# First two memory key products between the last three down products of the first feed-forward, with their results copied later

## The chip, the core and the metric

The kernel runs on one core of one Trainium2 chip. The metric is the device time of one execution in microseconds (us), and the median of several runs is compared. The core has five engines that work side by side, each through its own queue of instructions in order: TensorE (PE in the profile; its weight loads are PEld), VectorE (DVE), ScalarE (ACT), GpSimd (POOL) and SyncE (SP), which only starts transfers here. They meet through semaphores: an instruction adds to one, and another engine's queue stands still until a value is reached.

## The reference, cut to what matters

The program is a two layer hybrid block (`first_block`) and a second block with one layer (`second_block`), on 512 tokens of width 1024. All that the change touches lies in the second block's layer:

```python
def swiglu_ffn(x, w_in, w_down):
    a, b = jnp.split(x @ w_in, 2, axis=-1)
    return (jax.nn.silu(a) * b) @ w_down          # D_FF = 2816

def hybrid_layer_2(x, mem, ...):
    x = x + 0.5 * swiglu_ffn(rmsnorm(x, ffn1_norm), ffn1_w_in, ffn1_w_down)
    u = rmsnorm(x, mix_norm)
    proj = u @ w_in                               # u_ssm, q, k, v, xq, gates
    ...
    y_ssm = jax.nn.gelu(s5_scan(u_ssm, ssm_a_re, ...))
    ...
    br_mem = memory_cross_attention(xq, rmsnorm(mem, mem_norm), xattn_w_kv) @ xattn_w_up

def memory_cross_attention(xq, mem_n, w_kv):      # 256 memory rows, 4 heads of 128
    mk, mv = jnp.split(mem_n @ w_kv, 2, axis=-1)
    ...
```

The four key products `mk0` to `mk3` (one head each) and the value product `mvc0` depend on the memory alone. The mix norm depends on all eight down products of the first feed-forward.

## The kernel before

Activations lie with features on partitions: `xT` holds 8 blocks of 128 features by 512 tokens. Every float32 product is made of three rounded ones: the weight and the activation are each split into a rounded part (high) and the rest (low), and high by high, low by high and high by low are summed. A product over n blocks of 128 is thus 3n matmuls.

**The weight stream.** All weights lie in one stream of chunks of 128 x 1024, in the order of use. Three engines prepare a chunk: SP's transfer into one of RAW = 4 ring slots (`Weights.load`, L120), ACT's rounding into one of HIGH = 3 slots (`round`, L140; `round_one`, L149), POOL's subtraction in four pieces (`rest`, L170), which lie in the ring's slot. A transfer waits until the chunk four before it is used up by TensorE, a rounding until the chunk three before it is. ACT's `round(name)` stands at fixed places of ACT's queue and rounds what is due by then; `round_one` rounds one chunk, and waits for it there.

**The order around the change.** TensorE (`tensor`): eight down products `f1d0` to `f1d7`, 66 matmuls and 2.75 chunks each; behind `f1d1` the memory's sum of squares, behind `f1d5` `power_rows` (L2237), 64 small matmuls for the state space part. Then `mk0` (24 matmuls of 256 columns, one chunk), `norm_total` (the mix norm's sums over the partitions), `mk1`, `norm_spread` (its inverse root to all partitions), `mk2`, `mk3`, `mvc0` (48 matmuls, 4 chunks), `u0` to `u3` (24 matmuls, one chunk each; `u0` needs the mix norm's result), `q0`, `ssm_in`, `q1` to `q4`, `ssm_lags` (L2300, waits for DVE's `s_cw`), `q5`, and so on. Results go to two banks in turn (`proj`), and a product waits until the bank's last result is moved.

DVE (`vector`): the residual sums of the down products; `norm_scale` (L545) of the mix norm, eight times a scaling `hT` (L557) and a rest `h_low` (L551) that waits for ACT's `h_high`; then, for the state space part and without a wait on anything late, the powers of b (L3178 to L3183), `phase(0)` (L3196 to L3205), a memset and the powers of c (L3220 to L3233), the last of which raises `s_cw`; then the scan.

ACT (`scalar`): for each down product `ready(i)` rounds weights, waits for the residual sum and squares it. Then it moves `mk0`, takes the mix norm's root, and moves `mk1` to `mk3`, with two `norm_high` (L542) behind each. Then follow `round_one`, the last two `norm_high`, `mvc0`, `u0` to `u3`, and `table(0)` (L2703 to L2706), which waits for `phase(0)`.

POOL (`gpsimd`): the rests of the weights in order; behind `f1d7` it starts three transfers of 512 KB for the state space part.

The keys' place `mk` shares memory with the tail of the feed-forward's activations (`act_tail`), which the down products read to their end.

Of the kernel before, what the change touches and what calls it, by code (L numbers as in the profile page):

```python
# [10 lines left out]
ACT = mybir.ActivationFunctionType  # L11
AX = mybir.AxisListType

P = 128
T = 512
D = 1024
KD = D // P
# [56 lines left out]
class Weights:  # L74
# [109 lines left out]
    def product(self, pe, result, out, xs, tokens=False, ready=None):  # L184

        n = len(xs)
        for k, (xh, xl) in enumerate(xs):
            if ready is not None:
                ready(k)
            wh, wl = self.parts(pe, result, k)  # L190
            for i, (w, x) in enumerate(((wh, xh), (wl, xh), (wh, xl))):
                a, b = (x, w) if tokens else (w, x)
                mm = pe.matmul(out, a, b, start=(k == 0 and i == 0), stop=(k == n - 1 and i == 2))  # L193
            if (self.G.part + result, k) in self.inside:
                self.s_used.on(mm)
        self.G.close(mm)
# [164 lines left out]
def here(nc):  # L361

    return -(-nc.sbuf_base // 32) * 32
# [174 lines left out]
def norm_high(S, act, n, k):  # L538

    at = KD * NORMS.index(n)  # L540
    act.wait_ge(S.s_h.sem, at + k + 1)
    S.s_hh.on(act.activation(S.h_high[:, k, :], S.hT[:, k, :], ACT.Copy))  # L542
# [1193 lines left out]
KF = FF // P  # L1736
NP = KF - 2
X_TOTAL = 7
X_SQUARES = {j: (2 * j - 4, 2 * j - 3) for j in range(2, 6)}
X_INVERSE = {8: slice(0, HALF), 9: slice(HALF, T)}  # L1740
X_SCALE = 10
# [4 lines left out]
XH, XD, MEM = 4, 128, 256  # L1746
# [92 lines left out]
def block_tiles():  # L1839

    def ffn(n):
        t = []
        for i in range(KF):
            t += [(f"{n}a{i}", KD, P), (f"{n}b{i}", KD, P)]
        return t + [(f"{n}d{d}", KF, P) for d in range(KD)]
    t = ffn("f1") + [(f"mk{i}", KD, P) for i in range(XH)] + [("mvc0", KD, T)]
    t += [(f"{n}{i}", KD, P) for n, c in (("u", 4), ("q", 6), ("k", 6)) for i in range(c)]
    t += [("v_part0", KD, HALF)] + [(f"xq{i}", KD, P) for i in range(3)] + [("vc0", KD, T), ("xq3", KD, P)]
    for d in range(KD):
        t += [(f"g0{d}", KD, P), (f"glb{d}", 4, P), (f"gla{d}", 4, P)]  # L1850
    t += [(f"g1{d}", KD, P) for d in range(EARLY_GATES)]
    for d in range(KD):
        t += [(f"g1{d}", KD, P)] if d >= EARLY_GATES else []
        t += [(f"up{d}", 2, P), (f"g2{d}", KD, P), (f"xup{d}", 4, P)]
    return t + [(f"o{d}", KD, P) for d in range(KD)] + ffn("f2")
# [14 lines left out]
def block_groups():  # L1870

    def ffn(n, between=[]):
        g = [(f"ms_{n}", "a")] + [(f"{n}{x}{i}", OWN) for i in range(2) for x in "ab"]
        for j in range(NP):
            g += [("ms_x", OWN)] if n == "f1" and j == X_TOTAL else []
            g += [(f"{n}p{j + 2}", OWN)]
        g += [(f"{n}d0", "v"), (f"{n}d1", "v")] + between + [(f"{n}d{d}", "v") for d in range(2, KD)]
        return g if n == "f1" else g + [("ms_early", "a"), ("f2_late", OWN), ("ms_late", "a")]
    g = ffn("f1", [("ms_mem", "a")])
    g += [("mk0", "a"), ("ms_mix", "a")] + [(f"mk{i}", "a") for i in range(1, 4)] + [("mvc0", "a")]  # L1880
    g += [(f"u{i}", "a") for i in range(4)]
    g += [(f"{n}{i}", "a") for n, i in FILLERS]
    glu = [(n + str(d), e) for d in range(KD) for n, e in (("g0", "a"), ("glb", "a"), ("gla", "v"))]
    for p in range(PAIRS):
        for kind, n in DILATED[p]:
            if kind == "glu":
                g += glu[:n]
                glu = glu[n:]
            if kind == "L":
                g += [(f"lse{p}{i}", "a") for i in range(PATTERNS)]  # L1890
            if kind == "V":
                g += [(f"pv{p}{n}", "v")]
    assert not glu
    for h in range(XH):
        g += [(f"g1{h}", "a"), (f"xo{h}", "v")]
    for d in range(KD):
        g += [(f"g1{d}", "a")] if d >= EARLY_GATES else []
        g += [(f"up{d}", "v"), (f"g2{d}", "a"), (f"xup{d}", "v")]
    g += [(f"o{d}", "v") for d in range(KD)]
    g += ffn("f2")  # L1900
    return g

# [5 lines left out]
def second_block(nc, stack, S, A, scratch, out_dram, first_lead, spent):  # L1908
# [16 lines left out]
    xT, hT, h_parts, rstd, proj, att, G, W = S.xT, S.hT, S.h_parts, S.rstd, S.proj, S.att, S.G, S.W  # L1925
    vecs, halfpi, epsc = S.vecs, S.halfpi, S.eps
    s_a, s_v, s_ac, s_vc = S.s_a, S.s_v, S.s_ac, S.s_vc
# [5 lines left out]
    v = qkvx[:, 12:18, :].rearrange("p a b -> p (a b)").rearrange("p (a b) -> p a b", a=TB)  # L1933
    xq = qkvx[:, 18:22, :]
    mk_at, mk = here(nc), sb("mk", [P, XH, MEM])
    logits_at, logits = here(nc), sb("logits", [P, LALL])
# [9 lines left out]
    merged = big[:, 4:4 + KD, :]  # L1946
    memT = logits[:, T:T + KD * MEM].rearrange("p (a b) -> p a b", a=KD)
    memsq = nc.alloc_sbuf_tensor_at("b2_memsq", [P, KD, MEM], F32, offset=S.h_high_at)
    mem_root = hT[:, 0, 0:MEM]
    x_squares = qkvx[:, 14:14 + KD, :]  # L1950
    x_rstd = rstd[:]
# [51 lines left out]
    mem_low = rounded("mem_low", [P, KD, MEM], logits_at + 4 * T)  # L2003
    mem_high = rounded("mem_high", [P, KD, MEM], turned_at)
# [24 lines left out]
    def act_rest(i):  # L2029
# [22 lines left out]
    s_gh, s_gl, s_memh, s_meml, s_bh, s_bl, s_mgh, s_mgl = (sem(n) for n in (  # L2052
        "act_high act_low mem_high mem_low branch_high branch_low merged_high merged_low").split())
# [60 lines left out]
    def tensor(pe):  # L2114
# [19 lines left out]
        def pair_products(n):  # L2134

            for j in range(NP):
                if n == "f1" and j == X_TOTAL:
                    G.open(pe, "ms_x")
# [49 lines left out]
        def ffn(n, norm_name):  # L2188
            lead_product(S, pe, norm_name, f"{n}a0", 0, lead[n], f"ms_{n}")
            lead_product(S, pe, norm_name, f"{n}b0", 1, lead[n], f"ms_{n}")  # L2190
            lead_product(S, pe, norm_name, f"{n}a1", 2, lead[n], f"ms_{n}")
            lead_product(S, pe, norm_name, f"{n}b1", 3, lead[n], f"ms_{n}")
            pair_products(n)
            xs = [(act_high[:, i, :], act_rest(i)) for i in range(KF)]
            pe.wait_ge(s_gated.sem, s_gated.base + 2 * pair_of(n, NP - 2) + 2)
            base = 0 if n == "f1" else KF
            for d in range(KD):
                ready = (lambda i: pe.wait_ge(s_gl.sem, base + i + 1)) if d == 0 else None
                if (n, d) == ("f2", KD - 1):
                    last_products(xs)  # L2200
                    continue
                product(f"{n}d{d}", xs, ready)
                if n == "f1" and d == 1:
                    memory_sum()
                if n == "f1" and d == 5:
                    power_rows()

        def half_total(i):

# [27 lines left out]
        def power_rows():  # L2237

            pe.wait_ge(s_r.sem, 3)
            for block in range(BLOCKS):  # L2240
                for i, at in enumerate((19, 14)):
                    for q_ in range(4):
                        j = 4 * block + q_
                        mm = pe.matmul(att[i][32 * q_:32 * q_ + 32, block * P:(block + 1) * P],
                                       st[:, at, j:j + 1].to_broadcast([P, 32]), ident, start=True, stop=True)
            s_arow.on(mm)
# [7 lines left out]

        ffn("f1", "ffn1")

        pe.wait_ge(s_meml.sem, KD)
        mem_parts = [(mem_high[:, j, :], mem_low[:, j, :]) for j in range(KD)]
        for i in range(XH):
            product(f"mk{i}", mem_parts)  # L2260
            if i == 0:
                norm_total(S, pe, "mix", "ms_mix")
            if i == 1:
                norm_spread(S, pe, "mix")
        banks = [G.open(pe, "mvc0"), att[2]]
        for k_, (xh, xl) in enumerate(mem_parts):
# [274 lines left out]
    def scalar(act):  # L2541

        G.part = "b."
        def move(name, out, func=ACT.Copy, src=None, **kw):
            W.round(act, name)
            bank = G.whole(act, name)
            G.empty(act.activation(out, bank[:, :] if src is None else src(bank), func, **kw), name)
# [128 lines left out]
        pair_ffn("f1", "ffn1")  # L2676
        memory()
        def ready(i):
            W.round(act, f"f1d{i}")
            G.moved(act, f"f1d{i}")  # L2680
        norm_squares(S, act, "mix", ready)
        half = lambda b: b[:, 0:HALF]

        move("mk0", mk[:, 0, :], src=lambda b: b[:, 0:MEM])
        norm_root(S, act, "mix", "ms_mix")
        for i in range(1, XH):
            move(f"mk{i}", mk[:, i, :], src=lambda b: b[:, 0:MEM])
            norm_high(S, act, "mix", 2 * i - 2)
            norm_high(S, act, "mix", 2 * i - 1)
        W.round_one(act)  # L2690
        norm_high(S, act, "mix", 6)
        norm_high(S, act, "mix", 7)
        W.round(act, "mvc0")
        bank = G.whole(act, "mvc0")
        s_ac.on(act.activation(mv[:, 0, :], bank[:, :], ACT.Copy))
# [31 lines left out]
        for m, (n, i) in enumerate(FILLERS):  # L2727
# [12 lines left out]
            else:  # L2740
                g = 0 if n == "xq" else i // 2
# [62 lines left out]
        for p in range(PAIRS):  # L2804
            d = 4 * p
# [1063 lines left out]
```

## Time and profile before

| what | value |
|---|---|
| median of 3 runs | 2422.01 us (2421.76 to 2422.35) |
| the profiled execution, its own time | 2421.36 us |
| its span in the profile | 2419.3 us |
| TensorE busy | 2396.3 us, 99% of the span |
| VectorE busy | 1358.7 us, 56% |
| ScalarE busy | 1151.4 us, 48% |
| GpSimd busy | 1359.0 us, 56% |
| mean granted TensorE clock | 0.998 |

The times of a row are counted from the start of the span. A row's duration of a matmul includes the time to pass through the array and overlaps the next one; what a matmul costs in a row of them is the distance of the starts. In square brackets behind an instruction stands how long its engine was idle ahead of it, and what ended that.

### The profile page before, as it was taken

To read this page: it belongs to the slowest core of one execution; us is meant where nothing else is said; L and a number is where in the kernel's file an instruction comes from. 1 tells how busy PE (TensorE), PEld (TensorE's weight loads), DVE (VectorE), ACT (ScalarE), POOL (GpSimd) and SP (SyncE) were. 2 spreads that over 40 slices of the span, in tenths; PEclk is the share of its full clock that TensorE was granted. 3 is DMA by queue.
4 is the path that set the end of the run, shared out by engine and by line. 5 is a ranking of instruction groups with operands and counts; after the bars stand their busy time and mean duration, and the time that the engine had idled before them with its cause. 6 is when DMAs were issued, how large, how long until landed. Compare 5 with 4: busy or idle time off the path is not lost.

```text
span 2419.3 us, 36056 instructions
## 1 busy us (share of the span) xinstructions
PE 2396.3 (99%) x13834; PEld 2036.7 (84%) x13834; DVE 1358.7 (56%) x2527; ACT 1151.4 (48%) x1825; POOL 1359.0 (56%) x1774
## 2 busy tenths in 40 slices
PE   9999999999999999999999999999999999999998
PEld 6887788888788787888889998878988788899987
DVE  7965865222696576432387753199266433766502
ACT  5444676323534477532366553242366524555521
POOL 5553554555564454455586774584443455877753
PEclk9999999999999999999999999999999999999999
DMA  4232221233232212232223332332222233233332
GB/s 151 92 119 78 71 78 63 96 97 98 85 96 84 79 62 79 79 96 96 97 89 104 105 122 89 130 114 79 82 84 71 70 97 96 88 106 105 105 96 88
DMA packets 64423, 224.59 MB, mean 93 GB/s; under 512 B 7367, under 2 KB 10951, under 8 KB 64124
## 3 DMA queue, kind: packets, MB, share of 16 engines
q1 hardware_dynamic: 62620, 216.49, 28.0%
q0 software_dynamic: 1632, 5.78, 0.7%
q8 instruction: 111, 1.82, 0.3%
q14 instruction: 60, 0.49, 0.1%
HBM read 219.57 MB, written 3.99 MB: 92 GB/s over the span
## 4 chain that ended last, share of the span: by engine, by line
PE 90%; DVE 4%; POOL 3%; ACT 2%; DMA 1%; issue 1%; SPq 0%; DVEq 0%; ACTq 0%; POOLq 0%
PE proj L193 62%; PE proj L2157 9%; PE att L2157 7%; PE att L193 2%; PE proj L913 1%; PE att L892 1%; POOL b_x_low L3517 1%; PE att L1004 1%; POOL weight_low L170 1%; PE att L903 1%; PE att L991 1%; PE att L2346 1%; PE att L946 1%; POOL weight_low L3511 1%; DMA ring<-in_stream 1%; PE att L935 1%
## 5 line engine op out<-in xcount | busy, mean ns | idle before, releaser
L170 POOL TENSOR_TENSOR weight_low<-ring,weight_high 128x256 fp32r<-128x256 f32 x1272 | 999.7, 818 | 902.2 <-ACT weight_high L140 882.4
L193 PE MATMUL proj<-h_high,weight_high 128*128 128x512 f32 x1320 | 520.2, 394 | 0.7 <-POOL weight_low L170 0.6
L193 PE MATMUL proj<-h_low,weight_high 128*128 128x512 f32 x1320 | 514.1, 389 | 0.0
L193 PE MATMUL proj<-h_high,weight_low 128*128 128x512 f32 x1320 | 513.9, 389 | 0.0
L140 ACT ACTIVATE weight_high<-ring 128x1024 fp32r<-128x1024 f32 x313 | 329.7, 1054 | 302.8 <-PE proj L193 264.9
L193 PEld LDWEIGHTS proj<-h_high,weight_high 128*128 128x128 f32 x1320 | 247.8, 188 | 57.0 <-issue 4.2
L193 PEld LDWEIGHTS proj<-h_low,weight_high 128*128 128x128 f32 x1320 | 247.8, 188 | 52.2
L193 PEld LDWEIGHTS proj<-h_high,weight_low 128*128 128x128 f32 x1320 | 248.0, 188 | 49.4
L3511 POOL TENSOR_TENSOR weight_low<-ring,weight_high 128x256 fp32r<-128x256 f32 x240 | 191.6, 826 | 0.0
L193 PE MATMUL proj<-b_act_high,weight_high 128*128 128x512 f32 (+1 forms) x352 | 135.0, 384 | 0.0
L193 PE MATMUL proj<-b_act_high,weight_low 128*128 128x512 f32 (+1 forms) x352 | 134.7, 383 | 0.0
L1643 DVE TENSOR_TENSOR turned<-proj,probs 128x512 f32<-128x512 f32 x32 | 22.1, 692 | 189.4 <-PE proj L193 189.4
L2157 PE MATMUL proj<-b_x_T_high,h_low 128*128 128x256 f32 x640 | 119.1, 284 | 3.8 <-issue 3.8
L2990 DVE SCALAR_TENSOR_TENSOR xT<-proj,xT 128x512 f32<-128x512 f32 x15 | 10.4, 692 | 186.8 <-PE proj L193 186.8
L193 PE MATMUL proj<-b_act_low,weight_high 128*128 128x512 f32 (+1 forms) x288 | 110.2, 383 | 0.0
L3527 POOL TENSOR_TENSOR hT<-ring 128x256 f32<-128x256 f32 x80 | 58.2, 748 | 90.7 <-PE proj L2157 90.7
L2157 PEld LDWEIGHTS proj<-b_x_T_high,h_low 128*128 128x128 f32 x640 | 100.1, 193 | 4.2 <-issue 4.2
L2157 PE MATMUL proj<-b_x_T_low,h_low 128*128 128x256 f32 x320 | 90.8, 284 | 0.0
L193 PE MATMUL proj<-weight_high,h_high 128*128 128x256 f32 x288 | 82.4, 286 | 0.0
L193 PE MATMUL proj<-weight_high,h_low 128*128 128x256 f32 x288 | 81.5, 283 | 0.0
L193 PE MATMUL proj<-weight_low,h_high 128*128 128x256 f32 x288 | 81.5, 283 | 0.0
L193 PEld LDWEIGHTS proj<-b_act_high,weight_high 128*128 128x128 f32 x352 | 66.1, 188 | 13.1 <-issue 0.2
(618 smaller groups left out, 5636.9 us busy)
## 6 DMA issues: line engine op xcount, KB each, us to landing
ring<-in_stream SPq DMA_DIRECT2D x398, 512.0 KB, 3.5
xT<-in_x SPq DMA_DIRECT2D x4, 512.0 KB, 6.3
idx<-gate_rows POOLq DMA_DIRECT2D x8, 256.0 KB, 4.0
out<-hT SPq DMA_DIRECT2D x8, 256.0 KB, 2.3
bias_rows<-bias_row SPq DMA_DIRECT2D x2, 512.0 KB
b_logits<-in_mem POOLq DMA_DIRECT2D x1, 1024.0 KB, 5.0
bias_rows<-bias_row SPq DMA_DIRECT2D x1, 768.0 KB
consts<-in_const SPq DMA_DIRECT2D x1, 576.0 KB, 9.6
```

The source lines that it names most:

```text
L140: self.s_high.on(act.activation(self.high[:, c % HIGH, :], self.raw[:, c % self.slots, :], ACT.Copy))
L170: self.s_low.on(pool.tensor_tensor(self.low[:, c % self.slots, cols], self.raw[:, c % self.slots, cols], self.high[:, c % HIGH, cols], ALU ...
L193: mm = pe.matmul(out, a, b, start=(k == 0 and i == 0), stop=(k == n - 1 and i == 2))
L892: mm = pe.matmul(att[2 * bank + hh][:, col:col + WQ[b]], dq[rows(hh), p, b * P:(b + 1) * P], dk[rows(hh), p, 0:WQ[b]], start=True, stop=True)
L903: tr = pe.transpose(att[2 * bank + hh][:, col + (b - s) * P:col + (b - s + 1) * P], probs[:, hh, OQ[b] + s * P:OQ[b] + (s + 1) * P], ident)
L913: mm = pe.matmul(out[rows(hh), s * P:T], v[:, s, h * HD:(h + 1) * HD], turned[:, hh, KOFF[s]:KOFF[s] + WK[s]], start=(s == 0), stop=(s == ...
L935: mm = pe.matmul(att[3 * hh + bank][:, col:col + WQ[b]], sq_[rows(hh), p, b * P:(b + 1) * P], sk[rows(hh), p, 0:WQ[b]], start=True, stop=True)
L946: tr = pe.transpose(att[3 * hh + bank][:, col + (b - s) * P:col + (b - s + 1) * P], probs[:, hh, at:at + P], ident)
L991: mm = pe.matmul(att[3 * (h % 2) + bank][:, col:col + WK[s]], mk[:, h, s * P:(s + 1) * P], mq[:, h, s * P:T], start=True, stop=True)
L2157: mm = pe.matmul(out, w[:, cols], part[:, k, :], start=(first and k == 0 and i == 0), stop=(k == 3 and i == 2), skip_group_check=True)
L3511: signal.on(pool.tensor_tensor(out[:, cols], form[:, cols], high[:, cols], ALU.subtract))
L3527: s_sf3.on(pool.tensor_tensor(s_slot(3 * q_ + 1)[2][:, cols], W.raw[:, ca % RAW, cols], W.raw[:, cb % RAW, cols], ALU.subtract))
```

## The change

The weights of `mk0` are put behind those of `f1d5` in the stream, those of `mk1` behind `f1d6`, and the products stand there in TensorE's order; the other two keys stay behind `f1d7`. `power_rows` moves from behind `f1d5` to behind `f1d4`. The wait for the memory's rests (`s_meml`) moves ahead of `mk0`. ACT moves the two early results to `mk_early`, a free place in `logits`, and copies both to `mk` in one instruction behind the mix norm's root. `norm_total` now stands behind `mk2`, `norm_spread` behind `mk3`. On ACT, one `round_one` now stands ahead of all eight `norm_high`, and two more between them.

```diff
+EARLY_KEYS = {5: 0, 6: 1}
@@ block_tiles
-        return t + [(f"{n}d{d}", KF, P) for d in range(KD)]
-    t = ffn("f1") + [(f"mk{i}", KD, P) for i in range(XH)] + [("mvc0", KD, T)]
+        for d in range(KD):
+            t += [(f"{n}d{d}", KF, P)]
+            t += [(f"mk{EARLY_KEYS[d]}", KD, P)] if n == "f1" and d in EARLY_KEYS else []
+        return t
+    t = ffn("f1") + [(f"mk{i}", KD, P) for i in range(len(EARLY_KEYS), XH)] + [("mvc0", KD, T)]
@@ block_groups
-        g += [(f"{n}d0", "v"), (f"{n}d1", "v")] + between + [(f"{n}d{d}", "v") for d in range(2, KD)]
+        for d in range(KD):
+            g += [(f"{n}d{d}", "v")] + (between if d == 1 else [])
+            g += [(f"mk{EARLY_KEYS[d]}", "a")] if n == "f1" and d in EARLY_KEYS else []
-    g += [("mk0", "a"), ("ms_mix", "a")] + [(f"mk{i}", "a") for i in range(1, 4)] + [("mvc0", "a")]
+    g += [("mk2", "a"), ("ms_mix", "a"), ("mk3", "a"), ("mvc0", "a")]
@@ second_block
+    mk_early = logits[:, T + KD * MEM:T + KD * MEM + 2 * MEM].rearrange("p (a b) -> p a b", a=2)
@@ tensor, ffn
-                if n == "f1" and d == 5:
+                if n == "f1" and d == 4:
                     power_rows()
+                if n == "f1" and d in EARLY_KEYS:
+                    if d == min(EARLY_KEYS):
+                        pe.wait_ge(s_meml.sem, KD)
+                    product(f"mk{EARLY_KEYS[d]}", mem_parts)
@@ tensor
-        pe.wait_ge(s_meml.sem, KD)
-        for i in range(XH):
+        for i in range(2, XH):
             product(f"mk{i}", mem_parts)
-            if i == 0:
+            if i == 2:
                 norm_total(S, pe, "mix", "ms_mix")
-            if i == 1:
+            if i == 3:
                 norm_spread(S, pe, "mix")
@@ scalar
         def ready(i):
+            if i - 1 in EARLY_KEYS:
+                m = EARLY_KEYS[i - 1]
+                move(f"mk{m}", mk_early[:, m, :], src=lambda b: b[:, 0:MEM])
             W.round(act, f"f1d{i}")
             G.moved(act, f"f1d{i}")
         norm_squares(S, act, "mix", ready)
-        move("mk0", mk[:, 0, :], src=lambda b: b[:, 0:MEM])
+        move("mk2", mk[:, 2, :], src=lambda b: b[:, 0:MEM])
         norm_root(S, act, "mix", "ms_mix")
-        for i in range(1, XH):
-            move(f"mk{i}", mk[:, i, :], src=lambda b: b[:, 0:MEM])
-            norm_high(S, act, "mix", 2 * i - 2)
-            norm_high(S, act, "mix", 2 * i - 1)
+        G.moved(act, "mk1")
+        s_ac.on(act.activation(mk[:, 0:2, :], mk_early, ACT.Copy))
+        move("mk3", mk[:, 3, :], src=lambda b: b[:, 0:MEM])
         W.round_one(act)
-        norm_high(S, act, "mix", 6)
-        norm_high(S, act, "mix", 7)
+        for t in range(KD):
+            norm_high(S, act, "mix", t)
+            if t in (2, 5):
+                W.round_one(act)
```

## Rows read from the trace of the kernel before

**Rows 1.** The page, first part: busy time of each engine.

```profile
PE 2396.3 (99%) x13834; PEld 2036.7 (84%) x13834; DVE 1358.7 (56%) x2527; ACT 1151.4 (48%) x1825; POOL 1359.0 (56%) x1774
```

**Rows 2.** Busy time by stretch: length; PE, PEld, DVE, ACT, POOL; granted clock; DMA share.

```profile
1546.00:1562.00 16.00, 16.00 (x74) 13.28 (x73) 1.48 (x3) 3.26 (x4) 8.48 (x12) 1.00 0.29 99
1575.00:1590.00 15.00, 12.88 (x51) 8.79 (x51) 14.76 (x22) 7.11 (x10) 15.00 (x16) 1.00 0.43 144
```

**Rows 3.** Timeline of TensorE, from the first key product to the value product.

```profile
1561.55 0.28 PE L193 MATMUL proj<-b_mem_high,weight_high 128*128 128x256 f32 x1
...
1564.42 0.95 PE L516 MATMUL proj<-consts_all,rstd 128*128 128x1 f32 x8
...
1568.18 1.05 PE L524 MATMUL att<-consts_all,scal 128*128 128x128 f32 x8
...
1574.82 0.40 PE L2270 MATMUL proj<-weight_high,b_mem_high 128*128 128x512 f32 x1
```

**Rows 4.** The same timeline: the longest of five waits in the value product, and its end.

```profile
1579.05 0.50 PE L2270 MATMUL proj<-weight_high,b_mem_high 128*128 128x512 f32 x1 [0.86 <-POOL weight_low L170]
...
1589.44 0.39 PE L193 MATMUL proj<-h_high,weight_high 128*128 128x512 f32 x1
```

**Rows 5.** The chain that ended last, in order of time: start, length, what.

```profile
1564.62 6.86 DMA ring<-in_stream
...
1572.64 13.86 POOL weight_low L170 x14
1589.60 27.20 PE proj L193 x120
```

**Rows 6.** Timeline of ACT at the mix norm, and at the first table.

```profile
1570.05 1.29 ACT L542 ACTIVATE h_high<-hT 128x512 fp32r<-128x512 f32 x2 [1.29 <-DVE hT L557]
1571.50 1.06 ACT L140 ACTIVATE weight_high<-ring 128x1024 fp32r<-128x1024 f32 x1 [0.16 <-DMA ring<-in_stream]
...
1611.89 1.05 ACT L2703 ACTIVATE b_big<-b_big 128x1024 f32<-128x1024 f32 x1
```

**Rows 7.** Timeline of POOL, the rests of the weights behind the keys.

```profile
1572.64 28.98 POOL L170 TENSOR_TENSOR weight_low<-ring,weight_high 128x256 fp32r<-128x256 f32 x32 [2.83 <-ACT weight_high L140]
...
1617.40 8.95 POOL L170 TENSOR_TENSOR weight_low<-ring,weight_high 128x256 fp32r<-128x256 f32 x8 [4.03 <-ACT weight_high L140]
```

**Rows 8.** Busy time by stretch, as rows 2, cut at the stages of DVE's chain.

```profile
1569.25:1580.75 11.50, 10.44 (x66) 8.61 (x65) 11.28 (x16) 9.32 (x14) 8.67 (x9) 1.00 0.57 189
1580.75:1593.90 13.15, 12.08 (x50) 9.17 (x51) 12.98 (x19) 4.16 (x5) 13.15 (x16) 1.00 0.40 132
1593.90:1611.00 17.10, 17.10 (x78) 14.14 (x77) 16.59 (x27) 4.64 (x6) 14.27 (x18) 1.00 0.30 93
1612.70:1616.50 3.80, 3.80 (x19) 3.05 (x17) 3.73 (x8) 3.77 (x5) 0.67 (x1) 1.00 0.71 268
1616.50:1640.55 24.05, 24.05 (x218) 20.29 (x217) 23.81 (x25) 6.88 (x9) 19.25 (x18) 1.00 0.30 89
1664.90:1677.80 12.90, 12.90 (x170) 10.85 (x169) 12.76 (x27) 2.13 (x3) 5.94 (x8) 1.00 0.25 83
```

**Rows 9.** Timelines of DVE (state scalars, end of the powers of c) and of TensorE (`ssm_lags`).

```profile
1490.78 0.85 DVE L2944 TENSOR_TENSOR b_st<-b_st 128x16 f32<-128x16 f32 x2
...
1639.36 1.23 DVE L3233 TENSOR_TENSOR b_big<-b_big,b_qkvx 128x512 f32<-128x512 f32 x1
...
1642.50 1.95 PE L2307 MATMUL att<-b_big,b_qkvx 128*32 128x128 f32 x64
```

**Rows 10.** Timeline of TensorE behind its two longest idle times of one kind.

```profile
1232.11 0.48 PE L2157 MATMUL proj<-b_x_T_high,h_low 128*128 128x256 f32 x2 [1.90 <-issue]
...
2086.63 0.47 PE L2157 MATMUL proj<-b_x_T_high,h_low 128*128 128x256 f32 x2 [1.91 <-issue]
```

**Rows 11.** Busy time by stretch behind these two idle times, as rows 2.

```profile
1233.00:1237.00 4.00, 4.00 (x23) 4.00 (x22) 2.93 (x4) 1.33 (x2) 4.00 (x4) 0.57 0.01 4
...
2086.00:2090.00 4.00, 3.37 (x28) 3.40 (x29) 3.27 (x5) 2.14 (x5) 4.00 (x4) 1.00 0.02 4
```

More of the change, by code:

```diff
@@ L2204, in ffn @@
                     memory_sum()
-                if n == "f1" and d == 5:
+                if n == "f1" and d == 4:
                     power_rows()
+                if n == "f1" and d in EARLY_KEYS:
+                    if d == min(EARLY_KEYS):
+                        pe.wait_ge(s_meml.sem, KD)
+                    product(f"mk{EARLY_KEYS[d]}", mem_parts)
+        mem_parts = [(mem_high[:, j, :], mem_low[:, j, :]) for j in range(KD)]
         def half_total(i):
@@ L2255, in tensor @@
         ffn("f1", "ffn1")
-        pe.wait_ge(s_meml.sem, KD)
-        mem_parts = [(mem_high[:, j, :], mem_low[:, j, :]) for j in range(KD)]
-        for i in range(XH):
+        for i in range(2, XH):
             product(f"mk{i}", mem_parts)
-            if i == 0:
+            if i == 2:
                 norm_total(S, pe, "mix", "ms_mix")
-            if i == 1:
+            if i == 3:
                 norm_spread(S, pe, "mix")
```

## The prediction, made before the changed kernel was run

> **What bounds the kernel now.** The page's first part comes first: TensorE is busy for 2396.3 of 2419.3 us [rows 1], so all its waits together are worth 23 us. What the change is worth must be read from the stage that it edits. In the table by stretch, TensorE is full in the last down products (16.00 of 16.00 us), while in the value product behind them it works 12.88 of 15.00 us and POOL all 15.00 [rows 2]. The timeline gives the same wait in another way: `mvc0` lasts from 1574.82 to 1589.44 [rows 3, 4], 14.62 us. Its 48 matmuls cost 27.20 / 120 = 0.227 us each where nothing is late [rows 5], 10.88 us in all. So 3.7 us are lost there, in five waits for POOL, the longest 0.86 us [rows 4]. The chain that ended last says why: the transfer of the first value chunk took 6.86 us, and from 1572.64 the chain runs through POOL [rows 5], which needs 28.98 / 8 = 3.62 us for a chunk [rows 7] of which TensorE uses one in 10.88 / 4 = 2.72 us.
>
> Then comes the engine that seems far from critical. By stretch, DVE is busy without a break from the mix norm at 1569.25 to 1640.55: 11.28 of 11.50, 12.98 of 13.15, 16.59 of 17.10, 3.73 of 3.80 and 23.81 of 24.05 us [rows 8]. Its last instruction ends at 1639.36 + 1.23 = 1640.59, and `ssm_lags`, which needs it, starts on TensorE at 1642.50 [rows 9]. The chain has 1.9 us to spare, and no wait shows that today.
>
> **Part by part.** I write times of the changed kernel less the shift of the eighth down product's end as "shifted", to set them beside rows of before.
>
> *The moved products.* A key product takes 1564.42 - 1561.55 = 2.87 us [rows 3], the same in either place, since TensorE has no gaps in the downs [rows 2]: the end of `f1d7` moves 5.74 us later, and 5.74 us less work follows it. The wait for the memory's rests and the earlier `power_rows` cost nothing: DVE has finished both inputs by 1490.78 + 0.85 = 1491.6 [rows 9], some 20 us ahead of either. The result banks alternate as before, and a bank's move is covered by a key product or a down product.
>
> *The stall in the value product.* The first two value chunks are now rounded as `mk2` and `mk3` were, and POOL has both done by 1570 shifted, ahead of their use. The third takes the first one's place in time: its transfer waits for `mk2`, lands at 1571.48 shifted [rows 5], and POOL starts on it at 1572.64. TensorE, which starts `mvc0` at about 1569.0 (shifted, two keys earlier), uses the first two until 1574.5. It finds the first half of chunk three just done (two pieces of 3.62 / 4 us, 1574.45), waits some 0.4 us for the second half and as much for each half of chunk four, since 2.72 us of use stand against 3.62 us of POOL's. With the restarts I take 1.5 of the 3.7 us as left and 2.2 us as gained.
>
> *The vector chain.* It starts behind `norm_spread`, which stands behind two key products and `f1d7` as before. So it starts 5.74 us later, whatever the value product gains. Four terms follow.
> (1) Start: +5.74.
> (2) The norm's rests wait for ACT. Before, the first `h_high` ran at 1570.05, ahead of the rounding at 1571.50 that waited for the 6.86 us transfer [rows 6]. Now `round_one` stands ahead of all eight, and the first `h_high` starts at about 1571.50 + 1.06 = 1572.56. DVE has two scalings done by then and 14 of its 16 instructions of 11.50 / 16 = 0.72 us [rows 8] before it: 1573.2 + 10.1 = 1583.3 against 1580.75. The bounds are 0 and +2.5; I take +2.2, near the upper one, since DVE can't begin a rest sooner.
> (3) The powers of b (13.15 us under full POOL work [rows 8]) stay as they are. `phase` runs faster with less POOL work beside it: it takes 17.10 us with 14.27 us of POOL, its twin 12.90 us with 5.94 [rows 8], 0.50 us for each us of POOL. It would start at about 1596.1 shifted. POOL then has six chunks behind 1572.64 instead of eight, is done with them at 1595 and with the two of `q0` and `q1` at 1598 and 1603 (ACT rounds them when `u1` and `u2` are done): 5.4 us beside the phase, 12.6 us long, with the 0.4 us gap ahead of the memset 13.0. That is -4.1; the bounds are -7.1 (no POOL at all) and 0.
> (4) ACT's `table(0)`, at 1611.89 [rows 6] the first to wait for the phase, starts some 3 us later and holds up the roundings of `q2` and on. POOL's work on five chunks, from 1617.40 at 8.95 / 8 = 1.12 us a piece [rows 7], falls wholly into the powers of c: 22.4 us instead of 0.67 + 19.25 [rows 8], times 0.50: +1.2. The bounds are 0 and +2.5.
> The sum is 5.74 + 2.2 - 4.1 + 1.2 = +5.0. The chain ends at 1645.6, and `ssm_lags` starts 5.0 - 1.9 = 3.1 us later than before. TensorE would be there 2.2 us earlier, at 1640.3, and stands idle for 5.3 us: the gain in the value product is given back in full, with 3.1 us more. The rounding behind the table feeds `q2`, at 1623.7 by TensorE's new order, and is some 0.7 us early; if it were late, only the wait at `ssm_lags` would be shorter.
>
> *What comes behind.* From there the order is as before and shifted for both engines, for DVE 1.9 us more than for TensorE; I find no place there where DVE is needed within that. The copy of both keys, one ACT instruction of half a microsecond, lies in ACT's wait for the transfer. The end moves with `ssm_lags`.
>
> *The clock.* The trace has no idle time of 5 us in its middle. It has two of 1.9 us: behind the one that ends at 1232.11 the granted clock was 0.57 on average over 4.00 us, the lower level of 1.2 GHz for most of it; behind the one that ends at 2086.63 it stayed at 1.00 [rows 10, 11]. The first cost up to 4.00 x 0.43 = 1.7 us. For an idle time over twice as long I take 1.7; the bounds are 0 and 3.4, twice that. The Trainium skill ("TensorE: Matmul & The Clock Gate", Part 1: The HAM clock gate) says that an idle TensorE is put back to half its clock and gets the full one only after sustained work. By that rule the cost would fall due at `ssm_lags` and the sum would be that with it; the trace agrees in one of the two idle times.
>
> The sum is 3.1 + 1.7 = +4.8 us on the execution's own 2421.36, which gives 2426.2. The median of the runs is 0.65 us above that execution, so the forecast for a median is 2426.8.
>
> **Rivals.**
> A. The forecast: DVE's chain sets the start of `ssm_lags`, and the clock falls. 2426.8. For it: the chain without breaks [rows 8] and 1.9 us of slack [rows 9]. Against it: each of its terms beyond the first is an estimate.
> B. The same wait, but the clock stays up, as at 2086.63 [rows 11]: 2425.1. A wait this long speaks against it.
> C. Faster: DVE catches up. With little POOL work beside it, `phase` and the powers of c shrink until `s_cw` is there when TensorE arrives, at 1640.3; then the value product's 2.2 us stay, and the time is 2419.8. This decides from a chain that ends at least 0.3 us earlier than before's 1640.59, so terms 2 to 4 would have to make -6.0 where I count -0.7. At 0.50 us for each us, all of POOL's work beside both stages is worth some 17 us, so it can't be excluded, but the weights of `q0` to `q4` have to be made in that time.
> D. Clearly slower: POOL's relief in `phase` fails to come, as its two chunks for `q0` and `q1` or late ones of `u` fall into it after all. Then term 3 is about -1, the chain ends 8.1 us late, TensorE waits 6.2 us more than before, and with the clock the time is 2429.9.
> E. The moved products change neither: the wait for weights goes elsewhere by the same amount and DVE is not needed in time. 2422.0. The five waits for POOL [rows 4] and the moved norm speak against it.
>
> **How the numbers follow.** Chances: A 0.56, B 0.15, C 0.12, D 0.13, E 0.04. The forecast is A's, 2426.8. The range takes in B and D's middle and the bounds of the clock: 2423.0 to 2430.5; C, E and the far end of D stay outside, with some 0.2. About 0.2% is what a measurement of this kernel can tell from no change, that is 4.8 us, and A lies on that line: half of it counts as slower. Slower: 0.28 + 0.13 = 0.41. Faster by that much needs more than all of the 3.7 us in the value product: 0.02 of C. The same: the rest, 0.57.
>
> **What would show it.** In the changed kernel's profile: TensorE in `mvc0` with about 1.5 us of waits instead of 3.7; an idle time of 4 to 7 us ahead of `ssm_lags`, ended by DVE's last power of c, and this link in the chain that ended last; DVE without a break from the norm to it, its `phase` some 4 us shorter; ACT waiting for a transfer ahead of the first `h_high`; a granted clock below 1.00 in `ssm_lags` and `q5`. The prediction is wrong if TensorE has no wait at `ssm_lags` (C or E), or if a wait of more than 1 us shows in the downs, where I count none.

## The result, and the profile after

The changed kernel takes **2427.57 us** (median of 11 runs, 2426.97 to 2428.73), the kernel before 2421.76 us (2420.95 to 2422.35) beside it: a ratio of 1.0025, with an interval of 1.0017 to 1.0033. The change costs 5.8 us; the forecast was 2426.8 us, that is 4.8 us. The profiled execution is the longest of the eleven, 2428.73 us, span 2426.8 us.

Two rows place it against the rows of before. They are TensorE's idle times of 1.9 us of [rows 10], far ahead of the edit and far behind it.

Timeline of TensorE, changed kernel (start, length, engine, line, operation, tiles; in brackets the idle time before it and what ended it):

```profile
1233.00 0.47 PE L2164 MATMUL proj<-b_x_T_high,h_low 128*128 128x256 f32 x2 [1.90 <-issue]
...
2094.00 0.47 PE L2164 MATMUL proj<-b_x_T_high,h_low 128*128 128x256 f32 x2 [1.90 <-issue]
```

The first stands 1233.00 - 1232.11 = 0.89 us later than in [rows 10], the second 2094.00 - 2086.63 = 7.37 us. This execution thus brings 0.89 us along from ahead of the edit, and loses 6.48 us between the two. From here, "net" means less 0.89 us.

The same view at the start and the end of the value product, and at `ssm_lags`:

```profile
1575.66 0.47 PE L2281 MATMUL proj<-weight_high,b_mem_high 128*128 128x512 f32 x1
...
1584.57 0.50 PE L2281 MATMUL proj<-weight_high,b_mem_high 128*128 128x512 f32 x1 [0.18 <-POOL weight_low L170]
1586.41 0.50 PE L2281 MATMUL proj<-weight_high,b_mem_high 128*128 128x512 f32 x1 [0.17 <-POOL weight_low L170]
1589.01 0.47 PE L193 MATMUL proj<-h_high,weight_high 128*128 128x512 f32 x1 [0.96 <-POOL weight_low L170]
...
1647.49 3.64 PE L2318 MATMUL att<-b_big,b_qkvx 128*32 128x128 f32 x64 [5.23 <-DVE b_big L3248]
...
1651.65 0.63 PE L193 MATMUL proj<-h_high,weight_low 128*128 128x512 f32 x1
...
1657.42 3.85 PE L2305 MATMUL att<-b_uT,b_qkvx 32*128 32x128 f32 x128
```

And `ssm_in(1)` in the kernel before, beside [rows 9]:

```profile
1650.05 3.85 PE L2294 MATMUL att<-b_uT,b_qkvx 32*128 32x128 f32 x128
```

The value product begins at 1575.66 and `u0` at 1589.01: 13.35 us against 14.62 [rows 3, 4], 1.27 us gained. From `u0` to `ssm_lags` it is 58.48 us against 1642.50 - 1589.44 = 53.06 [rows 4, 9]: 5.42 us lost, and the row says to what: TensorE stood idle for 5.23 us until DVE's last power of c. `ssm_lags` itself lasts 3.64 us in place of 1.95 [rows 9], and a matmul of 128x512 right behind it takes 0.63 us. From `ssm_lags` to `ssm_in(1)` it is 9.93 us, against 1650.05 - 1642.50 = 7.55 in the kernel before: 2.38 us more. The filled wait below, where the clock is full, has 7.55 us too. The sum, -1.27 + 5.42 + 2.38 = 6.53, is the 6.48 us between the two markers.

Busy time by stretch, changed kernel (length; PE, PEld, DVE, ACT, POOL, each with its instructions; granted clock; DMA share, GB/s):

```profile
1590.60:1603.80 13.20, 13.20 (x60) 10.92 (x59) 13.03 (x19) 4.98 (x7) 13.20 (x16) 1.00 0.29 88
1603.80:1616.50 12.70, 12.70 (x60) 10.25 (x59) 12.26 (x27) 2.42 (x4) 7.68 (x10) 1.00 0.38 125
1616.50:1647.40 30.90, 25.75 (x224) 21.52 (x224) 30.52 (x32) 11.79 (x14) 22.61 (x20) 0.97 0.28 86
1640.00:1647.00 7.00, 2.25 (x10) 1.52 (x9) 6.90 (x9) 0.60 (x1) 4.35 (x4) 0.91 0.28 75
1647.00:1651.00 4.00, 3.51 (x64) 2.96 (x64) 4.00 (x13) 0.00 (x0) 0.00 (x0) 0.50 0.00 0
1651.00:1653.00 2.00, 2.00 (x9) 1.59 (x6) 1.97 (x7) 1.76 (x3) 0.00 (x0) 0.60 0.00 0
1653.00:1657.00 4.00, 4.00 (x19) 3.32 (x18) 3.97 (x5) 1.67 (x3) 2.21 (x3) 1.00 0.00 0
```

The first three rows are stages of DVE's chain, as in [rows 8]: DVE is busy in nearly all of each, and POOL works for 7.68 us beside the phase in place of 14.27. The last four are the clock: 0.50 for the four microseconds behind the idle time, the lower level of 1.2 GHz, and 1.00 again from 1653.

Timeline of DVE, changed kernel: the norm, then the starts of the powers of b, of the phase and of the memset behind it, and the last power of c:

```profile
1575.94 1.41 DVE L557 SCALAR_TENSOR_TENSOR hT<-xT,vecs_all,att 128x512 f32<-128x512 f32 x2 [2.72 <-PE att L524]
1579.41 0.82 DVE L551 TENSOR_TENSOR h_low<-hT,h_high 128x512 fp32r<-128x512 f32 x1 [2.07 <-ACT h_high L542]
1580.16 0.73 DVE L557 SCALAR_TENSOR_TENSOR hT<-xT,vecs_all,att 128x512 f32<-128x512 f32 x1
1580.82 1.26 DVE L551 TENSOR_TENSOR h_low<-hT,h_high 128x512 fp32r<-128x512 f32 x1
...
1584.51 1.25 DVE L551 TENSOR_TENSOR h_low<-hT,h_high 128x512 fp32r<-128x512 f32 x1
...
1586.34 0.68 DVE L551 TENSOR_TENSOR h_low<-hT,h_high 128x512 fp32r<-128x512 f32 x1
...
1590.62 0.67 DVE L3193 TENSOR_TENSOR b_qkvx<-b_qkvx,att 128x512 f32<-128x512 f32 x1
...
1603.81 3.52 DVE L3211 TENSOR_SCALAR b_turned<-consts_all,b_st 128x128 f32<-128x128 f32 x8
...
1616.57 1.76 DVE L3223 MEMSET b_logits<- 128x2048 f32 x1 [0.37 <-issue]
...
1646.75 0.69 DVE L3248 TENSOR_TENSOR b_big<-b_big,b_qkvx 128x512 f32<-128x512 f32 x1
```

And of ACT, where that 2.07 us wait comes from, and of POOL, up to the end of the phase:

```profile
1577.80 1.06 ACT L149 ACTIVATE weight_high<-ring 128x1024 fp32r<-128x1024 f32 x1 [2.37 <-DMA ring<-in_stream]
1578.77 1.14 ACT L542 ACTIVATE h_high<-hT 128x512 fp32r<-128x512 f32 x2
```

```profile
1578.94 7.42 POOL L170 TENSOR_TENSOR weight_low<-ring,weight_high 128x256 fp32r<-128x256 f32 x8 [2.47 <-ACT weight_high L149]
1588.11 17.85 POOL L170 TENSOR_TENSOR weight_low<-ring,weight_high 128x256 fp32r<-128x256 f32 x20 [1.75 <-ACT weight_high L149]
1607.27 3.38 POOL L170 TENSOR_TENSOR weight_low<-ring,weight_high 128x256 fp32r<-128x256 f32 x4 [1.31 <-ACT weight_high L140]
1610.59 2.20 POOL L3520 DMA_DIRECT2D b_big<-bias_rows  x3
```

The chain that ended last, changed kernel (start, length, what):

```profile
1571.29 6.49 DMA ring<-in_stream
1577.80 1.06 ACT weight_high L149
1579.41 0.82 DVE h_low L551
...
1646.75 0.70 DVE b_big L3248
1647.49 3.64 PE att L2318 x64
1651.13 6.36 PE proj L193 x24
```

In [rows 5] the chain went from the transfer to POOL and from POOL to TensorE at `u0`. Now it goes from the transfer of the third value chunk, which stands in the first one's place, to ACT's rounding, to the norm's first rest, and through DVE alone for 68 us, until it reaches TensorE at `ssm_lags`. The engine that had 1.9 us to spare has become the bound of this stretch.

### The profile page after: what moved, and what is told of

The parts are those of the page before. It is cut to its first block, busy times and chain, and to the rows that moved or that the text cites. A ratio compares the mean times of both kernels' runs of the same rounds, so it can differ in the third digit from the quotient of the medians.

```text
span 2426.8 us, 36057 instructions
## 1 busy us (share of the span) xinstructions
PE 2397.4 (99%) x13834; PEld 2037.2 (84%) x13834; DVE 1358.3 (56%) x2527; ACT 1152.8 (48%) x1826; POOL 1360.0 (56%) x1774
## 3 DMA queue, kind: packets, MB, share of 16 engines
q0 software_dynamic: 1632, 5.78, 0.8%
## 4 chain that ended last, share of the span: by engine, by line
PE 88%; DVE 7%; POOL 2%; ACT 2%; DMA 1%; issue 1%; SPq 0%; DVEq 0%; ACTq 0%; POOLq 0%
PE proj L193 60%; PE proj L2164 9%; PE att L2164 7%; PE att L193 2%; PE proj L913 1%; PE att L892 1%; POOL b_x_low L3532 1%; PE att L1004 1%; PE att L903 1%; PE att L991 1%; PE att L2357 1%; POOL weight_low L3526 1%; PE att L946 1%; DMA ring<-in_stream 1%; PE att L935 1%
```

## The experiments

Each time is a median of 11 or 12 runs, with the interval of its ratio to the kernel before (2421.63 us beside the first four, 2421.48 beside the next four, 2421.70 beside the last).

**Restore ACT's order, keep the early keys.** A round of the norm's high parts stands ahead of each rounding again.

```diff
-        W.round_one(act)
         for t in range(KD):
             norm_high(S, act, "mix", t)
-            if t in (2, 5):
+            if t in (1, 3, 5):
                 W.round_one(act)
```

> The changed kernel, but ACT makes the first two h_high of the mix norm ahead of the rounding that waits for the late transfer (roundings behind the second, fourth and sixth instead of ahead of the first and behind the third and sixth). Theory (the vector chain sets ssm_lags): the norm stage of DVE gets about 2.8 us shorter again, phase gets some of it back by more POOL work beside it, so ssm_lags starts about 2 us later than in the kernel before instead of 4.1, with an idle time of 3 to 4 us in front of it; the clock may or may not fall. Time 2424 to 2426.5. Rival (ACT's new order is the whole loss, the later norm costs nothing): no idle time at ssm_lags and a gain, about 2419.5.

Measured: 2424.0 us, ratio 1.0010 (1.0001 to 1.0019). Timelines of DVE and TensorE in this kernel:

```profile
1574.83 1.41 DVE L557 SCALAR_TENSOR_TENSOR hT<-xT,vecs_all,att 128x512 f32<-128x512 f32 x2 [2.42 <-PE att L524]
1576.28 0.69 DVE L551 TENSOR_TENSOR h_low<-hT,h_high 128x512 fp32r<-128x512 f32 x1
...
1585.59 0.68 DVE L3192 TENSOR_TENSOR b_qkvx<-b_qkvx,att 128x512 f32<-128x512 f32 x1
```

```profile
1644.47 1.96 PE L2318 MATMUL att<-b_big,b_qkvx 128*32 128x128 f32 x64 [2.81 <-DVE b_big L3247]
```

The time is the lower end of what was expected. The norm takes 1585.59 - 1574.83 = 10.76 us and has no wait for ACT; the idle time ahead of `ssm_lags` is 2.81 us, a little under the expected 3 to 4, and `ssm_lags` lasts 1.96 us at a granted clock of 1.00. By the medians some 3.5 of the 5.8 us hang on ACT's order, with the fall of the clock that its longer wait brings, and 2.4 on the moved keys themselves. The split is rough: the interval of the 2.4 goes from 0.2 to 4.6 us.

**Move the waiting step, not the work ahead of it.** `ssm_lags` goes one product later.

```diff
-SSM_STEPS = {1: [(IN, 0)], 5: [(LAGS, 0)], 6: [(IN, 1), (WITHIN, 0)], 8: [(OUT, 0)], 13: [(WITHIN, 1)], 17: [(OUT, 1)]}
-AFTER_MOVE = {4: "lags", 8: "table", 18: "gelu"}
+SSM_STEPS = {1: [(IN, 0)], 6: [(LAGS, 0), (IN, 1), (WITHIN, 0)], 8: [(OUT, 0)], 13: [(WITHIN, 1)], 17: [(OUT, 1)]}
+AFTER_MOVE = {5: "lags", 8: "table", 18: "gelu"}
```

> The changed kernel, but ssm_lags stands behind q5 instead of ahead of it (ACT's move of its result behind q5's move). Theory: TensorE comes to ssm_lags 5.4 us later, when the powers of c are just done; the idle time of 5.2 us and the fall of the clock vanish, and the 1.4 us gained in the value product and u0 are kept: about 2420.4. Rival (the early key products themselves, or anything ahead of ssm_lags, cost the time): about 2427.6 as without the edit.

Measured: 2426.68 us, ratio 1.0021 (1.0012 to 1.0030). The expectation fell. Timeline of TensorE, and a stretch (columns as above), in this kernel:

```profile
1648.56 1.96 PE L2318 MATMUL att<-b_big,b_qkvx 128*32 128x128 f32 x64 [1.09 <-DVE b_big L3248]
1653.86 5.48 PE L2305 MATMUL att<-b_uT,b_qkvx 32*128 32x128 f32 x128 [3.35 <-DVE b_big L3267]
```

```profile
1653.50:1657.50 4.00, 3.64 (x80) 3.64 (x84) 3.93 (x4) 0.59 (x1) 3.33 (x3) 0.64 0.01 4
```

The wait at `ssm_lags` shrank to 1.09 us, but `ssm_in(1)` behind it waits 3.35 us: it needs DVE's next stage, sixteen products that end 5.3 us after the last power of c, and nothing stands between the two steps any more. I had looked at one dependence and not at the next one on the same chain. The clock fell here, 0.64 over four microseconds, and `ssm_in(1)` lasts 5.48 us in place of 3.85.

**The same move in the kernel before,** as a control.

> The kernel before with the same later place of ssm_lags, as the control: there is no idle time at ssm_lags there, so the theory says 2421.8, no change. If the later place is worth something by itself, it shows here.

Measured: 2421.63 us, ratio 0.9999 (0.9991 to 1.0008). No cost of the moved step by itself can be seen.

**Fill the wait.** 24 matmuls whose result nobody reads stand ahead of the wait in `ssm_lags`; they are the only addition to the changed kernel, and its output doesn't depend on them.

```diff
+            for i in range(24):
+                xh, _ = h_parts[i % KD]
+                pe.matmul(att[4][:, :], xh[:, 0:P], xh, start=True, stop=True)
             pe.wait_ge(s_cw.sem, 1)
```

> The changed kernel with 24 matmuls of 512 columns, whose result nobody reads, ahead of the wait at ssm_lags (5.4 us of work, as long as the idle time). Theory (the clock falls in the idle time and costs about 2.4 us in ssm_lags and q5): the clock stays at 1.00, ssm_lags takes 1.95 us instead of 3.64 and q5 some 0.7 less, and the added work is hidden but for 0.2 us: about 2425.4. Rival (ssm_lags and q5 are slow for another reason, or the clock costs nothing): 2427.6 to 2427.8.

Measured: 2425.29 us, ratio 1.0016 (1.0007 to 1.0024). Timeline of TensorE, and two stretches (columns as above), in this kernel:

```profile
1640.86 5.60 PE L2315 MATMUL att<-h_high 128*128 128x512 f32 x24
1646.39 1.95 PE L2321 MATMUL att<-b_big,b_qkvx 128*32 128x128 f32 x64
```

```profile
1640.00:1647.00 7.00, 7.00 (x53) 5.63 (x55) 6.93 (x12) 0.60 (x1) 2.40 (x3) 1.00 0.21 75
1647.00:1651.00 4.00, 4.00 (x64) 3.35 (x53) 3.97 (x13) 2.49 (x5) 0.00 (x0) 1.00 0.00 0
```

With the idle time filled the clock stays at 1.00, `ssm_lags` lasts 1.95 us, and the kernel is 2427.57 - 2425.29 = 2.3 us faster although TensorE does 5.5 us of useless work. That is near the 2.38 us by which the trace prices the fall, but the close agreement is partly chance: in this execution DVE's chain was 1.05 us shorter than in the changed kernel's (70.45 against 71.50 us) and ended at 1645.47, so the filling ran on for 0.9 us behind it. What this run shows directly is the clock at 1.00 and 1.95 us in place of 3.64.

**All three steps one product later,** so that a product stands between `ssm_lags` and `ssm_in(1)`: in the changed kernel, with ACT's old order, and in the kernel before.

```diff
-SSM_STEPS = {1: [(IN, 0)], 5: [(LAGS, 0)], 6: [(IN, 1), (WITHIN, 0)], 8: [(OUT, 0)], 13: [(WITHIN, 1)], 17: [(OUT, 1)]}
+SSM_STEPS = {1: [(IN, 0)], 6: [(LAGS, 0)], 7: [(IN, 1), (WITHIN, 0)], 9: [(OUT, 0)], 13: [(WITHIN, 1)], 17: [(OUT, 1)]}
-AFTER_MOVE = {4: "lags", 8: "table", 18: "gelu"}
+AFTER_MOVE = {5: "lags", 8: "table", 18: "gelu"}
```

> The changed kernel with the three steps of the state space layer that wait for VectorE each one product later: ssm_lags ahead of the sixth product of the loop (1 earlier: fifth), ssm_in(1) and ssm_within(0) ahead of the seventh, ssm_out(0) ahead of the ninth, ScalarE's copy of the lags one move later. Theory (the whole loss is TensorE waiting for a late VectorE, at one dependence and then at the next): the wait of 1.1 us ahead of ssm_lags that the run with only ssm_lags moved showed stays, its wait of 3.35 us ahead of ssm_in(1) goes, because s_rot comes 5.3 us after s_cw and a product of 5.3 us now stands between; ssm_in(1) is 3.85 us long again and not 5.48. So 2426.7 - 3.35 - 1.6 = 2421.7 us (2420.5 to 2423.0). Rival (the loss is passed on along the chain, whatever stands where: the next dependence, ssm_out(0) or ScalarE's table, takes it): a new wait of over 2 us behind ssm_in(1), and 2424.5 us or more.

> As the kernel before it in this call, and ScalarE's order of the copies first (a row of the norm's high part ahead of each rounding, as in the run with the copies first). Theory: VectorE's chain is 3 us earlier than in the changed kernel, so none of the waits ahead of ssm_lags, ssm_in(1) and ssm_out(0) is over 0.5 us and no clock falls there; what is left of the change is the memory value product, whose waits are 1.9 us in place of 3.7. So 2421.6 - 1.8 = 2419.8 us (2418.8 to 2421.2), faster than both kernels. Rival (VectorE's chain isn't all of it, another loss of about 2.5 us stands elsewhere in the changed kernel): 2421.5 us or more, with no wait left at these steps.

> Control: the kernel before with the same steps one product later, and nothing else. There VectorE had 1.9 us in hand, so nothing waits less by it: 2421.6 us, within 0.7 us of the kernel before. If it is faster than before by over 1 us, a gain of the two kernels with the moved steps is not the change's.

Measured: 2423.05 us, ratio 1.0007 (0.9999 to 1.0015), in the changed kernel; 2420.87 us, 0.9997 (0.9989 to 1.0006), with ACT's old order; 2421.63 us, 0.9998 (0.9989 to 1.0006), in the kernel before. `ssm_lags` in the first and the second of them:

```profile
1648.50 1.96 PE L2318 MATMUL att<-b_big,b_qkvx 128*32 128x128 f32 x64 [1.87 <-DVE b_big L3248]
```

```profile
1647.58 1.95 PE L2318 MATMUL att<-b_big,b_qkvx 128*32 128x128 f32 x64
```

In the first a wait of 1.87 us is left, the one at `ssm_in(1)` is gone and the clock stays up. The time lies 1.3 us above the expected 2421.7, 0.8 of it in that wait, for which I had taken the 1.09 us of one other execution. In the second TensorE waits nowhere at these steps. Its 2420.87 us lie in the expected range (2418.8 to 2421.2) and can't be told from the kernel before, so the gain that was expected there, 2419.8 us, is not shown. No other loss of that size hides in the change: with the wait for DVE gone, the 5.8 us are gone.

**One rounding ahead of the norm, as in the change, in the kernel before.**

```diff
+        W.round_one(act)
         for i in range(1, XH):
             move(f"mk{i}", mk[:, i, :], src=lambda b: b[:, 0:MEM])
             norm_high(S, act, "mix", 2 * i - 2)
             norm_high(S, act, "mix", 2 * i - 1)
-        W.round_one(act)
```

> The kernel before with one part of the change alone: ScalarE's rounding of one weight piece stands ahead of the norm's first high part in place of behind the sixth; no early keys. This measures the term 'norm stage'. ScalarE has to wait for the piece's transfer (it landed at 1571.5 us in the trace of before), so the first high part starts at 1572.5 in place of 1570.05. Theory (ScalarE's order makes the norm stage longer): norm's scaling to its last low part takes 13.3 to 14.7 us in place of 11.5, VectorE uses up its 1.9 us and TensorE waits up to 1.3 us ahead of ssm_lags: 2422.0 us (2421.5 to 2423.2). Rival (the longer norm stage came from GpSimd beside VectorE in another phase of the two, and not from ScalarE's order): the stage stays under 12.3 us and the time at 2421.6.

Measured: 2425.21 us, ratio 1.0011 (1.0002 to 1.0020). The norm's part holds: from scaling to the last rest it takes 1584.50 - 1570.17 = 14.33 us against 11.48 in the kernel before. The time misses by 2 us or more, since I had not asked what else stands behind ACT. Timeline and stretches in this kernel's value product:

```profile
1580.19 0.50 PE L2270 MATMUL proj<-weight_high,b_mem_high 128*128 128x512 f32 x1 [1.54 <-POOL weight_low L170]
...
1586.35 0.50 PE L2270 MATMUL proj<-weight_high,b_mem_high 128*128 128x512 f32 x1 [2.64 <-POOL weight_low L170]
```

```profile
1584.00:1587.00 3.00, 0.65 (x3) 0.56 (x4) 2.97 (x5) 2.69 (x3) 2.12 (x4) 1.00 0.56 175
1587.00:1590.60 3.60, 3.60 (x11) 2.78 (x10) 3.56 (x4) 0.00 (x0) 3.60 (x4) 0.58 0.00 0
```

ACT's later roundings stand behind the high parts, these wait for a DVE that is now late, and so POOL and TensorE get the last value chunks late: waits of 1.54 and 2.64 us in place of 0.86 at most [rows 4], with a clock of 0.58 behind the second. The whole value product lasts 17.82 us. In the changed kernel the early keys cover this: two of its four chunks are rounded before the norm.

**The steps two products later, ACT's order as changed.**

```diff
-SSM_STEPS = {1: [(IN, 0)], 5: [(LAGS, 0)], 6: [(IN, 1), (WITHIN, 0)], 8: [(OUT, 0)], 13: [(WITHIN, 1)], 17: [(OUT, 1)]}
+SSM_STEPS = {1: [(IN, 0)], 7: [(LAGS, 0)], 8: [(IN, 1), (WITHIN, 0)], 10: [(OUT, 0)], 13: [(WITHIN, 1)], 17: [(OUT, 1)]}
-AFTER_MOVE = {4: "lags", 8: "table", 18: "gelu"}
+AFTER_MOVE = {6: "lags", 8: "table", 18: "gelu"}
```

> The changed kernel, ScalarE's order as in the change, with the steps of the state space layer that wait for VectorE two products later: ssm_lags ahead of the seventh, ssm_in(1) and ssm_within(0) ahead of the eighth, ssm_out(0) ahead of the tenth, the copy of the lags two moves later. With one product the wait ahead of ssm_lags was 1.87 us and the time 2423.05; the memory value product took 13.4 us against 13.8 to 14.6 in the kernel before. Theory (what the change gains is that 0.9 us, what it loses is the wait alone): no wait over 0.3 us at these steps, 2423.05 - 1.9 = 2421.2 us less what is in hand, so 2420.6 us (2419.8 to 2421.8). Rival (VectorE and ScalarE behind these steps become late in their turn, ssm_within(1) at the thirteenth product or the gates first): a wait of 1 us or more there, and 2422.0 us or more.

Measured: 2421.57 us, ratio 0.9996 (0.9987 to 1.0005). Timelines of TensorE and DVE, and a stretch (columns as above), in this kernel:

```profile
1653.97 1.95 PE L2318 MATMUL att<-b_big,b_qkvx 128*32 128x128 f32 x64
```

```profile
2081.76 8.66 DVE L3070 TENSOR_TENSOR b_x_T_low<-b_big,b_x_T_high 128x1024 fp32r<-128x1024 f32 x1
```

```profile
2096.00:2100.00 4.00, 4.00 (x23) 4.00 (x23) 2.04 (x3) 1.33 (x2) 1.43 (x2) 0.58 0.00 0
```

`ssm_lags` starts without a wait, as expected, with ACT's order as changed, so moving the steps is enough by itself. The time lies in the expected range (2419.8 to 2421.8), but the 0.9 us of gain in the value product did not come: it lasted 14.28 us in this execution. The profiled execution is the longest of the eleven, 2429.84 us. Its extra 8 us lie far behind the edit: one operation of DVE took 8.66 us, 1.77 in the changed kernel, and TensorE then stood idle for 8.79 us; why is not known. Neither this version nor the one at 2420.87 us can be told from the kernel before.

## Why the prediction came true, point by point

- **The bound that it named decided.** An idle time of 4 to 7 us ahead of `ssm_lags`, ended by DVE, was forecast; it is 5.23 us, forecast 5.3 (the agreement to 0.1 us is luck, see the idle time below). That it is the cause, and not only where the time shows, rests on the two versions that take the wait away and are back at the time of before (2420.87 and 2421.57 us), while moving the steps by one product in the kernel before changes nothing (2421.63 us).
- **Start of DVE's chain: forecast +5.74.** Scaling starts at 1575.94 against 1569.27: 6.67, net 5.78. Right.
- **Norm: forecast +2.2, bound +2.5.** It took 1590.62 - 1575.94 = 14.68 us against 11.48: +3.2, outside the bounds. This is the mis-sized term. The wait for ACT was sized rightly, 2.07 us. Missing was that three of the rests shown singly took 1.25 us where only one of before's did: 2 x 0.57 = 1.1 us. The forecast had taken 0.72 us for each of them. In the run with only `ssm_lags` moved, with the same order of ACT, one rest took 1.27 us, and the stage 13.21 us.
- **Powers of b: forecast 0.** 13.19 us against 13.15. Right.
- **Phase: forecast -4.1.** From 1603.81 to 1616.57 are 12.76 us against 17.10 [rows 8]: -4.34. Of POOL's 7.68 us beside it 2.20 are the start of three transfers (L3520). The rests of the weights are 1605.96 - 1603.81 + 3.38 = 5.53 us in place of 14.27, forecast 5.4; and 4.34 / (14.27 - 5.53) = 0.50 us for each us of them, as forecast. Right, and so rival D is out.
- **Memset and powers of c: forecast +1.2.** 1647.44 - 1616.57 = 30.87 us against 1640.59 - 1611.00 = 29.59: +1.28, with POOL's five chunks as one block of 22.61 us (forecast 22.4). Right; rival C, that DVE catches up, is out, and with the wait at `ssm_lags` so is E.
- **The sum** of DVE's chain is +5.96 net against the forecast +5.0. The whole error is the norm.
- **The value product: forecast 2.2 us of 3.7 gained.** 1.27 us here, and less on average. The waits inside it are nearly gone (0.18 and 0.17 us), but `u0` waits 0.96 us for a chunk of its own: POOL started on it at 1588.11, because ACT's third rounding stood behind the norm's sixth high part. I had followed ACT's order to the first of its roundings only. Since TensorE waited for DVE anyway, this error cost nothing in the sum.
- **The clock: forecast 1.7, bound 3.4.** 2.38 us by the trace, roughly the same by the filled wait. The size was taken from an idle time less than half as long. Rival B is out.
- **The idle time: forecast 5.3.** That it is 5.23 us is luck. DVE's chain ended 0.96 us later than forecast, and TensorE, with 1.27 us gained in place of 2.2, came 0.93 us later: the two errors cancel in the wait. They don't cancel in the time, which goes by the chain.
- **In this execution** the terms were -1.27, +5.42 and +2.38, that is 6.5 us, where the forecast had -2.2, +5.3 and +1.7, that is 4.8. The 1.7 us between are the norm's 1.0 and the clock's 0.7. The medians differ by 5.8 us, less than this execution, so the forecast came nearer to the median than its terms to this trace.

**What one profile could not give.** The stages of DVE's chain were read from one execution. The experiments add five that can be paired; here they stand by where the steps of the state space layer are, in us (the powers of b, 13.15 to 13.20 us everywhere, left out):

| kernel | norm | phase | memset and powers of c | chain |
|---|---|---|---|---|
| before | 11.48 | 17.10 | 29.59 | 71.3 |
| changed | 14.68 | 12.76 | 30.87 | 71.5 |
| changed, wait filled | 13.04 | 13.33 | 30.88 | 70.5 |
| before, `ssm_lags` later | 12.52 | 16.86 | 30.29 | 72.8 |
| changed, `ssm_lags` later | 13.21 | 13.32 | 32.92 | 72.7 |
| before, three steps later | 13.95 | 15.91 | 30.72 | 73.7 |
| changed, three steps later | 14.69 | 12.76 | 32.94 | 73.6 |

The norm varies by 2.5 us in the order of before alone, yet at equal places of the steps the whole chain is as long with the change as without, to within 0.2 us (0.9 with the filled wait). The three terms behind the start, -0.7 us by the forecast, come to nothing: what the norm and the powers of c lose, the phase gives back. So the shift is the 5.74 us of the two keys, less 1.9 us of slack, 3.8 us; with the clock's 2.38 that is 6.2, where the medians say 5.8. That the terms cancel holds with ACT's order as changed: with its old order beside the early keys the chain is 69.6 us, against 71.3 in the kernel before, and 70.1 with the three steps later, against 73.7 (one execution each). There the early keys shorten the chain, and the new order of ACT takes that back. The wait of 1.87 us that the three moved steps left, against 1.09 us with `ssm_lags` alone, is in it too: 14.69 + 12.76 are 0.92 us more than 13.21 + 13.32. The value product lasted 14.6, 14.3 and 13.8 us in the three executions with the order of before, and 13.4, 13.3, 13.2, 13.4 and 14.3 us in the five with that of the change: a gain of 0.75 us between the means. Why one execution differs from the next by that much was not tried.

## What to carry to other kernels

Work that is moved ahead of a stage delays everything that this stage starts, on every engine: before the gain at the next wait is counted, follow the longest chain that begins there to the place where it is needed again, and compare the delay with its slack there. If that wait is then taken away by moving the waiting step, ask the same of the next step on the chain. Where an engine issues both the roundings that feed one consumer and the copies that feed another, putting one first can make the other late (here the norm's first rest, by 2.07 us), and through it the engine's own later items (the waits of 1.54 and 2.64 us); follow all of its queue, not the first item.

## What the hardware showed beyond that

- **The clock.** On TensorE the lower level followed an idle time of 5.23 us (0.50 over four us) and one of 3.35 us (0.64 over four us, `ssm_in(1)` 5.48 us in place of 3.85), and one of 8.79 us far behind the edit in the last version (0.58 from 2096 to 2100 us, 1.4 us behind its end). It did not follow one of 2.81 us, and followed one of 2.64 us (0.58 over 3.6 us) that stood 6 us behind a wait of 1.54 us. The idle time of 1.90 us behind which it showed in [rows 11] left the clock at 1.00 in the changed kernel. The rule of the Trainium skill that the prediction cites ("TensorE: Matmul & The Clock Gate", Part 1: The HAM clock gate), that an idle TensorE is put back to half its clock, agrees with these three long ones; below them the length of an idle time alone did not tell.
- **DVE beside POOL.** The rest of a norm row (L551) takes 0.68 us or 1.25 us, while the scaling between them (L557) stays at 0.73 us. In the changed kernel the three long ones shown singly stand in POOL's block of 1578.94 to 1586.36, and the one at 1586.34, behind it, took 0.68. The last four powers of c, behind POOL's block that ends at 1644.35, took 0.68 or 0.69 us, where those within it took 1.1 to 1.2. But in the version with ACT's old order six of the eight rests took 0.68 or 0.69 us, although POOL worked beside most of them (14 pieces in 13.86 us from 1578.20, 0.99 us each, against 7.42 / 8 = 0.93 in the changed kernel). So POOL's presence alone doesn't say which of the two engines pays. The Trainium skill ("SBUF — State Buffer", SBUF: two separate sides) says that a DVE operation with two inputs in SBUF and a GpSimd operation that reads SBUF lock each other out, and that whichever starts first holds the ports for the whole instruction: the two lengths agree with that; no run here tries what decides which of the two starts first.
